# The second pair of output-projection tiles made of seven block products in place of eight

## The chip, the cores and the metric

The kernel runs on one core of one Trainium2 chip. The metric is the time of one execution on the device in microseconds (us), as the median of several runs. The engines are named as the profile names them: PE is TensorE (PEld its weight loads), DVE is VectorE, ACT is ScalarE, POOL is GpSimd and SP is SyncE, which only issues DMAs here.

## The reference

One decoder layer for 512 prompt tokens and 8 sample tokens (520 columns), in float32. What bears on this case is the end of the token mixer, where the merged branches go through the output projection onto the residual, and the norm behind it:

```python
x = x + (jax.nn.sigmoid(ga) * y_a + jax.nn.sigmoid(gb) * y_b) @ w_o
xn = rmsnorm(x, g2)
up = xn @ w_up
```

`w_o` is 1024 x 1024.

## The kernel before

**Tiles and slots.** Activations lie feature by feature: 8 blocks of 128 features (KT = 8) by 520 tokens (TOK), in two halves of 260 (HALF). A weight tile of 128 outputs by 1024 inputs is one slot; slots run in one fixed order and alternate between two buffers of everything (`raw`, `whi`, `wlo`, and the PSUM tiles `out_ps`, each with one bank for each half). Each float32 product is made of three fp32r products, high x high, high x low and low x high, so a slot takes 8 blocks x 3 x 2 halves = 48 matmuls of 128 x 128 by 260 columns. SP loads the raw weights of a slot; ACT's `split` rounds them to `whi`; DVE's `low` subtracts to get `wlo`; PE runs the slot (`tile`); DVE or ACT empties the PSUM tile (semaphores `evac`).

**The seven-product pairs.** Four tiles of the branch before (the gate slots of class `Pair`, two pairs) are already made this way: two output tiles, two halves of the inputs and two halves of the tokens make a 2 x 2 by 2 x 2 block product, which takes seven block products (`product`, 4 blocks x 3 = 12 matmuls each) in place of eight. For this DVE makes four sums of weight blocks (`weight_sums` into `wsum`), ACT and DVE split seven factors into high and low (`factor_hi`, `factor_low`, semaphores `factor_hi` and `factor_lo`), and x needs four combinations of its quarters (`tf`, split into `th` and `tl`). The products go to several PSUM places and DVE adds them up. The tile that follows a pair, `branch_tile`, takes its weights in two halves as places in `whi` and `wlo` come free.

**The output projection.** Its slots are S_WO to S_WO + 7, one for each output block j. Its input is `merged` (float32, 8 blocks), split block by block into `mh` and `ml`; the first tile waits for these block by block. For each j, DVE adds PSUM and residual (`xres`) into `x1`, which gives the semaphore s_x1; ACT multiplies by a gain into `x2h`, DVE makes the low part `x2l`. Between the two DVE makes the low weights of slot j + 2.

**POOL beside it.** POOL loads small constants for the next stage, stores `out_conv_old`, makes `sconv` of four operations, and then for each j squares `x1` (`sqa`) and adds it up (`acc`). After 6 of 8 blocks of the first tile of the next stage (S_UP), PE sums `acc` over the partitions (`norm_sums`) and so waits for all eight.

Order on each engine is the order of its program; there is no scheduler.

## Time and profile before

| | |
|---|---|
| median of 3 runs | 907.07 us (906.8 to 907.54) |
| the profiled execution, whole time | 906.57 us |
| its span, first to last instruction | 904.4 us |
| PE busy | 896.8 us, 99% |
| DVE busy | 548.9 us, 61% |
| ACT busy | 373.4 us, 41% |
| POOL busy | 136.2 us, 15% |

The span is what the trace covers; the profiled execution's own time is 2.17 us longer. Start times in rows count from the start of the span. Busy PE is not PE at its peak, since matmuls are pipelined; the distance from one matmul's start to the next tells the pace.

### The profile page before, as it was taken

How to read it: one execution, taken by the hardware profiler on the slowest of the kernel's cores; microseconds unless marked ns; L12 is line 12 of the kernel's file. 1: busy time of each engine (PE TensorE's matmuls, PEld its weight loads, DVE VectorE, ACT ScalarE, POOL GpSimd, SP SyncE). 2: the span in 40 equal slices, each digit the busy share in tenths (PEclk: the TensorE clock that was granted, in tenths of full speed). 3: DMA queues.
4: the chain of work that ended last, by engine and by line, in shares of the span. 5: the costliest groups of instructions: out<-in, count | busy, mean ns of one | idle time of the engine just before them, and what ended most of it. 6: DMA issues, size and time to landing. Idle time of an engine off the chain costs nothing.

```text
span 904.4 us, 19408 instructions
## 1 busy us (share of the span) xinstructions
PE 896.8 (99%) x7378; PEld 892.7 (99%) x7378; DVE 548.9 (61%) x863; ACT 373.4 (41%) x580; POOL 136.2 (15%) x182
## 2 busy tenths in 40 slices
PE   9999999999999999999999999999999999999997
PEld 9999999999999999999999999999999999999997
DVE  7895774442885444396755687777777777433234
ACT  7545434535863323243332344444444444322222
POOL 0682000011541111000006700000000000000001
PEclk9999999999999999999999999999999999999999
DMA  6332252234862222222254222222222222323322
GB/s 212 120 115 94 70 219 87 71 122 139 316 243 71 75 83 75 93 92 71 93 208 125 93 78 92 89 90 93 93 93 93 93 93 88 98 86 96 96 85 95
DMA packets 31489, 100.30 MB, mean 111 GB/s; under 512 B 4668, under 2 KB 7260, under 8 KB 31192
## 3 DMA queue, kind: packets, MB, share of 16 engines
q1 hardware_dynamic: 29256, 92.96, 30.7%
q0 software_dynamic: 1472, 5.72, 2.1%
q10 hardware_dynamic: 720, 1.04, 0.3%
q8 instruction: 29, 0.48, 0.2%
q14 instruction: 12, 0.10, 0.0%
HBM read 92.37 MB, written 7.35 MB: 110 GB/s over the span
## 4 chain that ended last, share of the span: by engine, by line
PE 91%; POOLq 3%; issue 3%; DMA 1%; POOL 1%; DVEq 0%; ACT 0%; DVE 0%; SPq 0%; ACTq 0%
PE out L1713 86%; PE trp L1713 2%; POOLq L1691 2%; PE aux L1713 1%; POOLq L1689 1%; PE trp L1745 1%; DMA cwb<-in_conv_wb 1%; DMA raw_pair<-in_w_slots 0%; PE aux L1902 0%; POOL y L1704 0%; POOL out_conv_old L1675 0%; POOL sct L1679 0%; DVEq L1530 0%; ACT whi L527 0%; POOLq L1682 0%
## 5 line engine op out<-in xcount | busy, mean ns | idle before, releaser
L971 DVE TENSOR_TENSOR wlo<-raw_pair,whi 128x1024 fp32r<-128x1024 f32 (+1 forms) x139 | 174.5, 1255 | 193.1 <-ACT whi L527 192.8
L527 ACT ACTIVATE whi<-raw_pair 128x1024 fp32r<-128x1024 f32 (+3 forms) x156 | 155.0, 997 | 251.8 <-PE out L1713 249.3
L1713 PE MATMUL out<-xh,whi 128*128 128x260 f32 x728 | 152.7, 288 | 0.0
L1713 PE MATMUL out<-xh,wlo 128*128 128x260 f32 x728 | 148.6, 283 | 0.0
L1713 PE MATMUL out<-xl,whi 128*128 128x260 f32 x728 | 148.5, 283 | 0.0
L1713 PE MATMUL out<-x2h,wlo 128*128 128x260 f32 x704 | 142.0, 283 | 0.0
L1713 PE MATMUL out<-x2h,whi 128*128 128x260 f32 x704 | 142.0, 283 | 0.0
L1713 PE MATMUL out<-x2l,whi 128*128 128x260 f32 x704 | 141.8, 283 | 0.0
L1713 PEld LDWEIGHTS out<-xh,whi 128*128 128x128 f32 x728 | 113.5, 189 | 0.5
L1713 PEld LDWEIGHTS out<-xh,wlo 128*128 128x128 f32 x728 | 113.1, 189 | 0.0
L1713 PEld LDWEIGHTS out<-xl,whi 128*128 128x128 f32 x728 | 113.0, 188 | 0.0
L1713 PEld LDWEIGHTS out<-x2h,whi 128*128 128x128 f32 x704 | 108.7, 189 | 0.1
L1713 PEld LDWEIGHTS out<-x2h,wlo 128*128 128x128 f32 x704 | 108.6, 189 | 0.0
L1713 PEld LDWEIGHTS out<-x2l,whi 128*128 128x128 f32 x704 | 108.3, 188 | 0.0
L1713 PE MATMUL out<-acth,whi 128*128 128x260 f32 (+2 forms) x338 | 70.7, 283 | 0.0
L1713 PE MATMUL out<-acth,wlo 128*128 128x260 f32 (+2 forms) x338 | 70.7, 283 | 0.0
L1713 PE MATMUL out<-actl,whi 128*128 128x260 f32 (+2 forms) x338 | 70.5, 283 | 0.0
L1489 DVE TENSOR_TENSOR up<-out,rbc 128x520 f32<-128x520 f32 x44 | 30.9, 702 | 42.1 <-PE out L1713 42.0
L1713 PEld LDWEIGHTS out<-acth,whi 128*128 128x128 f32 x338 | 53.1, 189 | 0.0
L1713 PEld LDWEIGHTS out<-acth,wlo 128*128 128x128 f32 x338 | 53.2, 189 | 0.0
L1713 PEld LDWEIGHTS out<-actl,whi 128*128 128x128 f32 x338 | 53.1, 188 | 0.0
L1697 POOL COPY nconv<-up 128x10 f32 x44 | 8.9, 203 | 242.9 <-DVEq L1490 242.9
(311 smaller groups left out, 1474.8 us busy)
## 6 DMA issues: line engine op xcount, KB each, us to landing
raw_pair<-in_w_slots SPq DMA_DIRECT2D x123, 512.0 KB, 3.3
raw_pair<-in_w_dn SPq DMA_DIRECT2D x16, 448.0 KB, 3.3
c_ring<-in_C_state SPq DMA_DIRECT2D x8, 512.0 KB, 4.9
row<-scratch SPq DMA_DIRECT2D x8, 512.0 KB, 5.9
out_C_sample<-c_ring SPq DMA_DIRECT2D x8, 512.0 KB, 4.2
raw_pair<-in_w_dn SPq DMA_DIRECT2D x8, 512.0 KB, 3.6
xres<-in_x_all POOLq DMA_DIRECT2D x1, 1560.0 KB, 6.9
x<-in_x_all SPq DMA_DIRECT2D x5, 260.0 KB, 6.5
```

The lines of the kernel that those rows point to most:

```text
L527: return act.activation(out, in_, func, **kw_)
L971: TT(wlo[p][:, 0:width], raw[p][:, 0:width], whi[p][:, 0:width].bitcast(F32), ALU.subtract)\
L1489: TT(both(up[t][:, 2:2 + TOK]), out2(n), both(rbc2[:, :]), ALU.mult).then_inc(evac[n.c % 2], 1)
L1689: pool.drain()
L1691: pool.drain()
L1697: pool.tensor_copy(nconv[:, i * 2 + t, :], up[t][:, SEQ:2 + TOK]).then_inc(s_nc, 1)
L1713: return pe.matmul(*a, **k)
L1745: m = pe.transpose(trp[b.c % 2][:, c, :], ftmp[b.c % 2][:, c * P:(c + 1) * P], ident[:, :])
```

## The change

Output tiles j = 2 and 3 (slots S_WO + 2 and + 3) become a pair of seven products (`OutPair`). Tiles 0, 1 and 4 to 7 stay as they were, tile 4 (slot S_WO + 4) with its weights in halves (`halves_tile`, which is `branch_tile` with its inputs as arguments). The input combinations are made anew, from the fp32 tiles of `merged`: four differences of 4 blocks x 260 columns on DVE (`merged_difference`), their high parts on ACT (`merged_combination_hi` into `mth`), their low parts on DVE (`merged_combination_low` into `tl`). The first difference and its high part lie inside the last gate pair, the three others behind it, ahead of the sum of tile 0. The loops of the projection are written out on PE, DVE and ACT. On SP, the loads of S_WO + 4 and + 5 wait for the factors made of the buffers that they overwrite. POOL's program stays the same.

```diff
+        class OutPair(Pair):
+            def __init__(self):
+                self.q = (KT - PLAIN) // 2
+                self.j = 2
+                self.n = [At(S_WO + 2 + t) for t in range(4)]
+                self.t0, self.t1 = self.n[0].c % 2, self.n[1].c % 2
+                self.p1, self.p6 = (trp[t][:, :, :].rearrange("p a b -> p (a b)")[:, 0:HALF] for t in range(2))
+                self.p5, self.p7 = (aux[:, t, 0:HALF] for t in range(2))
+                r0, r1 = raw[self.t0], raw[self.t1]
+                self.a11, self.a12, self.a21, self.a22 = r0[:, 0:HW], r0[:, HW:], r1[:, 0:HW], r1[:, HW:]
+                self.factor = (self.a11, self.a12, wsum[:, 3, :], wsum[:, 1, :], wsum[:, 0, :], wsum[:, 2, :], self.a22)
+
+        pair_o = OutPair()
...
-            load_slots(S_WO, S_DN)
+            load_slots(S_WO, S_WO + 4)
+            sp.wait_ge(s_sw, 4 * pair_o.q + 4)
+            sp.wait_ge(s_pl, 7 * pair_o.q + 2)
+            sp.dma_start(raw[pair_o.t0][:, :], wp[S_WO + 4]).then_inc(w_loaded[pair_o.t0], 16)
+            sp.wait_ge(s_pl, 7 * pair_o.q + 7)
+            sp.dma_start(raw[pair_o.t1][:, :], wp[S_WO + 5]).then_inc(w_loaded[pair_o.t1], 16)
+            load_slots(S_WO + 6, S_DN)
...
+            def merged_combination_hi(r, at):
+
+                act.wait_ge(s_bt, 4 + at)
+                A(mth[r][:, :, :], tf[:, r, :, :]).then_inc(s_th, 1)
...
                 if last:
                     split(At(S_WO + 1))
+                    merged_combination_hi(0, 1)
                 else:
                     next_factors_hi(pairs_w[q + 1])
                 merged_hi(pr.j + 1)
...
+            def out_pair(pr):
+                q, n = pr.q, pr.n
+                act.wait_ge(w_loaded[pr.t0], n[0].half(1) * 16)
+                act.wait_ge(done, n[0]())
+                factor_hi(pr, 0)
+                factor_hi(pr, 1)
+                second_hi(0)
+                act.wait_ge(s_sw, 4 * q + 4)
+                act.wait_ge(done, n[1]())
+                factor_hi(pr, 2)
+                factor_hi(pr, 3)
+                act.wait_ge(s_pd, 6 * q + 1)
+                factor_hi(pr, 4)
+                second_hi(1)
+                A(wtmp[1], pr.p1).then_inc(s_or, 1)
+                act.wait_ge(s_pd, 6 * q + 2)
+                factor_hi(pr, 5)
+                act.wait_ge(s_pd, 6 * q + 3)
+                act.wait_ge(w_loaded[pr.t1], n[1].half(1) * 16)
+                factor_hi(pr, 6)
+                act.wait_ge(w_loaded[pr.t0], n[2].half(1) * 16)
+                act.wait_ge(s_pd, 6 * q + 5)
+                A(whi[pr.t0][:, 0:HW], raw[pr.t0][:, 0:HW]).then_inc(s_nh, 1)
+                act.wait_ge(s_pd, 6 * q + 6)
+                A(whi[pr.t0][:, HW:], raw[pr.t0][:, HW:]).then_inc(w_hi, 3)
+                split(n[3])
+
+            merged_combination_hi(2, 2)
+            merged_combination_hi(1, 3)
+            merged_combination_hi(3, 4)
+            out_pair(pair_o)
+            second_hi(2)
+            second_hi(3)
...
+            def merged_quarter(k, h):
+
+                return merged[:, k * KT // 2:(k + 1) * KT // 2, h * HALF:(h + 1) * HALF]
+
+            def merged_difference(r, a, b):
+
+                TT(tf[:, r, :, :], a, b, ALU.subtract).then_inc(s_bt, 1)
+
+            def merged_combination_low(r, at):
+
+                dve.wait_ge(s_th, 4 + at)
+                TT(tl[:, r, :, :], tf[:, r, :, :], mth[r][:, :, :].bitcast(F32), ALU.subtract).then_inc(s_tl, 1)
+
...
                 if last:
                     low(At(S_WO))
+                    merged_difference(0, merged_quarter(0, 1), merged_quarter(0, 0))
                     merged_low(pr.j)
                 else:
...
+                dve.wait_ge(s_x2h, j + 1)
+                STT(x2l[:, j, :], x1[:, j, :], gains[:, 2, j:j + 1], x2h[:, j, :].bitcast(F32),
+                    ALU.mult, ALU.subtract).then_inc(s_x2, 1)
+
+            def first_sum(n, j):
+
+
+                return TT(both(x1[:, j, :]), out2(n), both(xres[:, j, :]), ALU.add).then_inc(evac[n.c % 2], 1)
+
+            def first_result():
+
+                dve.drain()
+                dve.nop().then_inc(s_x1, 1)
+
+            def out_pair(pr):
+                q, n, j = pr.q, pr.n, pr.j
+                part = lambda t, h: x1[:, j + t, h * HALF:(h + 1) * HALF]
+                rest = lambda h: xres[:, j + 1, h * HALF:(h + 1) * HALF]
+                ready(At(S_WO))
+                first_sum(At(S_WO), 0)
+                first_result()
+                merged_combination_low(0, 1)
+                merged_combination_low(2, 2)
+                factor_low(pr, 0)
+                factor_low(pr, 1)
+                weight_sums(pr)
+                ready(At(S_WO + 1))
+                first_sum(At(S_WO + 1), 1)
+                first_result()
+                factor_low(pr, 2)
+                second_low(0)
+                factor_low(pr, 3)
+                merged_combination_low(1, 3)
+                factor_low(pr, 4)
+                factor_low(pr, 5)
+                merged_combination_low(3, 4)
+                second_low(1)
+                dve.wait_ge(s_xrest, 16)
+                dve.wait_ge(s_pd, 6 * q + 3)
+                first_sum(n[0], j)
+                factor_low(pr, 6)
+                dve.wait_ge(s_or, 1)
+                dve.drain()
+                TT(part(0, 0), part(0, 0), wtmp[1], ALU.add)
+                dve.wait_ge(s_pd, 6 * q + 4)
+                TT(wtmp[0], wtmp[1], pr.p6, ALU.add)
+                dve.wait_ge(s_nh, q + 1)
+                TT(wlo[pr.t0][:, 0:HW], raw[pr.t0][:, 0:HW], whi[pr.t0][:, 0:HW].bitcast(F32), ALU.subtract).then_inc(s_nl, 1)
+                dve.wait_ge(s_pd, 6 * q + 5)
+                dve.drain()
+                TT(wtmp[1], wtmp[0], pr.p5, ALU.add)
+                dve.wait_ge(w_hi, n[2](1))
+                TT(wlo[pr.t0][:, HW:], raw[pr.t0][:, HW:], whi[pr.t0][:, HW:].bitcast(F32), ALU.subtract).then_inc(w_lo, 3)
+                dve.wait_ge(s_pd, 6 * q + 6)
+                dve.drain()
+                TT(wtmp[0], wtmp[0], pr.p7, ALU.add)
+                TT(part(0, 1), part(0, 1), wtmp[1], ALU.add)
+                first_result()
+                low(n[3])
+                ready(n[1])
+                TT(part(1, 0), rest(0), wtmp[0], ALU.add)
+                TT(part(1, 1), rest(1), wtmp[0], ALU.add)
+                dve.drain()
+                TT(part(1, 0), part(1, 0), out_ps[pr.t1][:, 0, 0:HALF], ALU.add).then_inc(evac[pr.t1], 1)
+                TT(part(1, 1), part(1, 1), pr.p5, ALU.add)
+                first_result()
+                second_low(2)
+                second_low(3)
+
+            dve.drain()
+            merged_difference(2, merged_quarter(1, 1), tf[:, 0, :, :])
+            merged_difference(1, merged_quarter(1, 1), merged_quarter(0, 1))
+            dve.drain()
+            merged_difference(3, merged_quarter(1, 0), tf[:, 2, :, :])
             dve.wait_ge(s_xres, 16)
-            wo_step(0)
-            dve.wait_ge(s_xrest, 16)
-            with dve.Fori(1, KT // 2) as i:
-                wo_step(i)
+            out_pair(pair_o)
+            for j in range(4, KT):
+                n = At(S_WO + j)
+                ready(n)
+                first_sum(n, j)
+                first_result()
+                low(n.plus(2))
+                second_low(j)
 
             def hidden_low(i):
 
@@ -1956,7 +2103,7 @@
                 pe.wait_ge(s_u2, q + 1)
...
             tile(At(S_WO + 1), mh, ml)
-            with pe.Fori(1, 4) as i:
-                for t in range(2):
-                    tile(At(S_WO + t, i, 2), mh, ml)
+
+            def merged_product_quarter(k, h):
+
+                part = (slice(None), slice(k * KT // 2, (k + 1) * KT // 2), slice(h * HALF, (h + 1) * HALF))
+                return mh[part], ml[part]
+
+            def merged_combination(r):
+
+                return mth[r][:, :, :], tl[:, r, :, :]
+
+            def out_pair(pr):
+                n = pr.n
+                product(pr, 0, pr.p1, *merged_product_quarter(0, 0)).then_inc(s_pd, 1)
+                pe.wait_ge(evac[pr.t0], n[0].half(1))
+                product(pr, 1, out_ps[pr.t0][:, 0, 0:HALF], *merged_product_quarter(1, 0)).then_inc(s_pd, 1)
+                product(pr, 2, out_ps[pr.t0][:, 1, 0:HALF], *merged_product_quarter(1, 1)).then_inc(s_pd, 1)
+                pe.wait_ge(s_tl, 4 + 2)
+                product(pr, 3, pr.p6, *merged_combination(2)).then_inc(s_pd, 1)
+                product(pr, 4, pr.p5, *merged_combination(0)).then_inc(s_pd, 1)
+                pe.wait_ge(s_tl, 4 + 3)
+                product(pr, 5, pr.p7, *merged_combination(1)).then_inc(s_pd, 1)
+                pe.wait_ge(s_tl, 4 + 4)
+                pe.wait_ge(evac[pr.t1], n[1].half(1))
+                product(pr, 6, out_ps[pr.t1][:, 0, 0:HALF], *merged_combination(3)).then_inc(done, 2)
+
+            out_pair(pair_o)
+            halves_tile(pair_o, mh, ml)
+            for j in range(5, KT):
+                tile(At(S_WO + j), mh, ml)
```

On DVE, this stood from the last operation of the branch to the low part of tile 1 of the projection (`x_94<-out,xres` is the sum of a tile, `wlo_119<-raw_pair,whi_117 128x1024` the low weights of a slot, `ml` the low part of a block of `merged`):

```order
L1339 TENSOR_TENSOR ml<-merged,mh 128x520 [waits merged_hi]
L1456 TENSOR_TENSOR x_94<-out,xres 128x520 [waits slots_done,residual_loaded]
L971 TENSOR_TENSOR wlo_119<-raw_pair,whi_117 128x1024 [waits w_hi]
L1461 SCALAR_TENSOR_TENSOR x2l<-x_94,gains,x2h 128x520 [waits x2_hi]
L1456 TENSOR_TENSOR x_94<-out,xres 128x520 [waits slots_done]
L971 TENSOR_TENSOR wlo_118<-raw_pair,whi_116 128x1024 [waits w_hi]
L1461 SCALAR_TENSOR_TENSOR x2l<-x_94,gains,x2h 128x520 [waits x2_hi]
```

And this stands there now, behind `ml<-merged,mh` and a first `tf<-merged,tf`, up to the factor that the third product takes (`tf` is a difference of `merged`, `tl<-tf,mth` its low part, `wlo ... 128x512` the low part of a factor, `wsum` the weight sums):

```order
L1430 TENSOR_TENSOR tf<-merged 128x1040
L1430 TENSOR_TENSOR tf<-merged,tf 128x1040
L1540 TENSOR_TENSOR x_94<-out,xres 128x520 [waits slots_done,residual_loaded]
L1435 TENSOR_TENSOR tl<-tf,mth_114 128x1040 [waits x_combinations_hi]
L1435 TENSOR_TENSOR tl<-tf,mth_116 128x1040 [waits x_combinations_hi]
L1411 TENSOR_TENSOR wlo_123<-raw_pair,whi_121 128x512 [waits factor_hi] x2
L1417 TENSOR_TENSOR wsum<-raw_pair 128x512 [waits w_loaded0,w_loaded1]
L1419 TENSOR_TENSOR wsum<-wsum,raw_pair 128x512
L1420 TENSOR_TENSOR wsum<-raw_pair 128x512
L1422 TENSOR_TENSOR wsum<-raw_pair,wsum 128x512
L1540 TENSOR_TENSOR x_94<-out,xres 128x520 [waits slots_done]
L1411 TENSOR_TENSOR wlo_122<-wsum,whi_120 128x512 [waits factor_hi]
```

Ahead of the sum of tile 0 stand three differences (two of them shown), and between the sums of tiles 0 and 1 two low parts of combinations, two factors and the four weight sums, where one `wlo` of a slot and one `x2l` stood.

Farther on DVE, from the factor of the fifth product to the two halves of the low weights of slot S_WO + 4 (`wlo ... [waits branch_half_hi]` and `[waits w_hi]`), all new:

```order
L1411 TENSOR_TENSOR wlo_123<-wsum,whi_121 128x512 [waits factor_hi] x2
L1435 TENSOR_TENSOR tl<-tf,mth_117 128x1040 [waits x_combinations_hi]
L1534 SCALAR_TENSOR_TENSOR x2l<-x_94,gains,x2h 128x520 [waits x2_hi]
L1540 TENSOR_TENSOR x_94<-out,xres 128x520 [waits products_done,residual_rest_loaded]
L1411 TENSOR_TENSOR wlo_122<-raw_pair,whi_120 128x512 [waits factor_hi]
L1576 TENSOR_TENSOR x_94<-x_94,ftmp_127 128x260 [waits out_product_copied]
L1578 TENSOR_TENSOR ftmp_127<-ftmp_127,trp 128x260 [waits products_done]
L1580 TENSOR_TENSOR wlo_123<-raw_pair,whi_121 128x512 [waits branch_half_hi]
L1583 TENSOR_TENSOR ftmp_127<-ftmp_127,aux 128x260 [waits products_done]
L1585 TENSOR_TENSOR wlo_123<-raw_pair,whi_121 128x512 [waits w_hi]
```

The factor of the seventh product (`wlo_122<-raw_pair,whi_120 128x512`) comes behind a low part, an `x2l` and a sum; the first half of the low weights of S_WO + 4 comes two more operations later.

On PE the tiles of the projection followed each other; this is the start of one in the loop (`out<-mh,whi`: high inputs, high weights):

```order
L1981 ISA
L1720 REGISTER_ALU [waits w_lo]
L1713 MATMUL out<-mh,whi_117 128x260 [waits bank_emptied1]
L1713 MATMUL out<-mh,whi_117 128x260
L1713 MATMUL out<-ml,whi_117 128x260 x2
L1713 MATMUL out<-mh,wlo_119 128x260 x2
```

Now the seventh product stands there, twelve matmuls on the last combination, of which the first three and the last are shown, and then tile 4:

```order
L1860 MATMUL out<-mth_117,whi_120 128x260 [waits factor_lo,bank_emptied0,x_combinations_lo]
L1860 MATMUL out<-tl,whi_120 128x260
L1860 MATMUL out<-mth_117,wlo_122 128x260
...
L1860 MATMUL out<-tl,whi_120 128x260
L1860 MATMUL out<-mth_117,wlo_122 128x260
L1860 MATMUL out<-mh,whi_121 128x260 [waits bank_emptied1,branch_half_lo]
```

A product of 12 matmuls now waits for a factor of its own, and the tile behind it for the first half of its low weights.

## Rows read from the trace of the kernel before

**Rows 1.** First part of the page: busy time of the engines.

```profile
PE 896.8 (99%) x7378; PEld 892.7 (99%) x7378; DVE 548.9 (61%) x863; ACT 373.4 (41%) x580; POOL 136.2 (15%) x182
```

**Rows 2.** Busy time over the projection's eight tiles (from:to length, engines' busy us, clock).

```profile
467.40:513.50 46.10, 46.10 (x386) 46.10 (x385) 27.30 (x25) 14.21 (x16) 29.77 (x23) 1.00 0.47 140
```

**Rows 3.** Timeline of PE: first matmuls of S_WO and of S_UP (start, length).

```profile
467.39 0.41 PE L1713 MATMUL out<-mh,whi 128*128 128x260 f32 x2
...
513.52 0.40 PE L1713 MATMUL out<-x2h,whi 128*128 128x260 f32 x2
```

**Rows 4.** Timeline of DVE: in the gate pairs, sums, factors, weight sums.

```profile
430.14 0.43 DVE L1408 TENSOR_TENSOR gtmp<-gtmp,out 128x260 f32<-128x260 f32 x1
...
441.69 1.29 DVE L1344 TENSOR_TENSOR wlo<-raw_pair,whi 128x512 fp32r<-128x512 f32 x2
442.89 0.69 DVE L1350 TENSOR_TENSOR wsum<-raw_pair 128x512 f32<-128x512 f32 x1
443.67 0.69 DVE L1352 TENSOR_TENSOR wsum<-wsum,raw_pair 128x512 f32<-128x512 f32 x1
...
445.06 0.69 DVE L1355 TENSOR_TENSOR wsum<-raw_pair,wsum 128x512 f32<-128x512 f32 x1
```

**Rows 5.** Combinations of x, high on ACT, low on DVE (ns min/median/max).

```profile
L527 ACT ACTIVATE th<-tf x4: 1053/1059/1062, 397.1 to 404.4; 128x1040 fp32r<-128x1040 f32 x4
L1327 DVE TENSOR_TENSOR tl<-tf,th x4: 1233/1234/1236, 404.5 to 410.5; 128x1040 fp32r<-128x1040 f32 x4
```

**Rows 6.** Timeline of DVE in the first two projection tiles (idle time before, and releaser).

```profile
473.42 0.70 DVE L1456 TENSOR_TENSOR x<-out,xres 128x520 f32<-128x520 f32 x1 [2.60 <-PE out L1713]
...
475.59 0.75 DVE L1461 SCALAR_TENSOR_TENSOR x2l<-x,gains,x2h 128x520 fp32r<-128x520 f32 x1
479.12 0.70 DVE L1456 TENSOR_TENSOR x<-out,xres 128x520 f32<-128x520 f32 x1 [2.77 <-PE out L1713]
480.21 1.25 DVE L971 TENSOR_TENSOR wlo<-raw_pair,whi 128x1024 fp32r<-128x1024 f32 x1 [0.39 <-ACT whi L527]
481.39 1.34 DVE L1461 SCALAR_TENSOR_TENSOR x2l<-x,gains,x2h 128x520 fp32r<-128x520 f32 x1
```

**Rows 7.** Timeline of POOL beside the projection.

```profile
477.42 2.07 POOL L1675 DMA_DIRECT2D out_conv_old<-cst  x1 [7.98 <-DMA cwb<-in_conv_wb]
479.43 0.95 POOL L1678 TENSOR_TENSOR sconv<-cst,cwb 128x352 f32<-128x352 f32 x1
480.25 1.92 POOL L1679 TENSOR_TENSOR sct<-cst,cwb 128x352 f32<-128x352 f32 x1
487.40 1.20 POOL L1681 TENSOR_TENSOR sconv<-sconv,cwb 128x352 f32<-128x352 f32 x1 [5.23 <-issue]
488.75 0.94 POOL L1683 TENSOR_TENSOR sconv<-sconv,sct 128x352 f32<-128x352 f32 x1
...
490.30 1.05 POOL L1688 TENSOR_TENSOR sqa<-x 128x520 f32<-128x520 f32 x1
491.50 1.31 POOL L1690 TENSOR_TENSOR acc<-acc,sqa 128x520 f32<-128x520 f32 x1
492.95 1.85 POOL L1688 TENSOR_TENSOR sqa<-x 128x520 f32<-128x520 f32 x1
...
514.66 1.05 POOL L1688 TENSOR_TENSOR sqa<-x 128x520 f32<-128x520 f32 x1 [1.71 <-DVEq L1457]
```

**Rows 8.** Timeline of DVE beside the rows of POOL from 490 us.

```profile
491.75 2.13 DVE L971 TENSOR_TENSOR wlo<-raw_pair,whi 128x1024 fp32r<-128x1024 f32 x1 [0.28 <-ACT whi L527]
493.81 1.55 DVE L1461 SCALAR_TENSOR_TENSOR x2l<-x,gains,x2h  x1
```

**Rows 9.** Sixth part of the page: the load of a slot (us to landing).

```profile
raw_pair<-in_w_slots SPq DMA_DIRECT2D x123, 512.0 KB, 3.3
```

**Rows 10.** Busy time at the span's end, PE idle (granted clock after the engines).

```profile
900.00:901.00 1.00, 0.00 (x0) 0.00 (x0) 0.95 (x4) 0.00 (x0) 1.00 (x2) 1.00 0.43 139
901.00:902.00 1.00, 0.00 (x0) 0.00 (x0) 0.00 (x0) 0.00 (x0) 0.21 (x1) 0.53 1.06 352
```

More of the change, by code:

```diff
@@ L60 @@
 PLAIN = 4
+OUT_PAIRS = 1
 HW = KT * P // 2
@@ L174, in hybrid_layer @@
         assert Q0 + 41152 + 16 * HW <= 165952
+        mth = [at("mth0", [P, KT // 2, HALF], Q0 + 2 * XB, F32R)]
+        mth += [at(f"mth{r}", [P, KT // 2, HALF], 4 * XB + XB // 4 * (r - 1), F32R) for r in range(1, 4)]
+        assert 4 * XB + 3 * XB // 4 <= F0
         acth = at("acth", [P, FT, TOK], Q0, F32R)
@@ L386, in hybrid_layer @@
         s_gs = sem("gate_sigmoids")
+        s_or = sem("out_product_copied")
         s_nh = sem("branch_half_hi")
@@ L860, in _, with second_hi @@
                 ay_pair(pr)
-            with act.Fori(0, KT // 2) as i:
-                for t in range(2):
-                    n = At(S_WO + t, i, 2)
-                    split(n.plus(2))
-                    apart()
-                    act.wait_ge(s_x1, i * 2 + (t + 1))
-                    A(x2h[:, i * 2 + t, :], x1[:, i * 2 + t, :], scale=gains[:, 2, bass.ds(i * 2 + t, 1)]).then_inc(s_x2h, 1)
+            def second_hi(j):
+                act.wait_ge(s_x1, j + 1)
+                A(x2h[:, j, :], x1[:, j, :], scale=gains[:, 2, j:j + 1]).then_inc(s_x2h, 1)
+            def out_pair(pr):
[31 more added lines that the diff above has]
+            for j in range(4, KT):
+                split(At(S_WO + j + 2))
+                second_hi(j)
             def up_step(i, first=False, last=False):
@@ L1448, in _ @@
                 ay_pair(pr)
-            def wo_step(i):
-                for t in range(2):
-                    n = At(S_WO + t, i, 2)
-                    j = i * 2 + t
-                    ready(n)
-                    TT(both(x1[:, j, :]), out2(n), both(xres[:, j, :]), ALU.add).then_inc(evac[n.c % 2], 1)
-                    dve.drain()
-                    dve.nop().then_inc(s_x1, 1)
-                    low(n.plus(2))
-                    dve.wait_ge(s_x2h, i * 2 + (t + 1))
-                    STT(x2l[:, j, :], x1[:, j, :], gains[:, 2, bass.ds(j, 1)], x2h[:, j, :].bitcast(F32),
-                        ALU.mult, ALU.subtract).then_inc(s_x2, 1)
@@ new lines, in _ @@
+            dve.drain()
[3 more added lines that the diff above has]
+            merged_difference(3, merged_quarter(1, 0), tf[:, 2, :, :])
+            dve.wait_ge(s_xres, 16)
+            out_pair(pair_o)
+            for j in range(4, KT):
+                n = At(S_WO + j)
[4 more added lines that the diff above has]
+                second_low(j)
@@ L1967, in branch_tile @@
                     w = slice(k * P, (k + 1) * P)
-                    for wt, x in ((whi[pr.t0], hah), (whi[pr.t0], hal), (wlo[pr.t0], hah)):
+                    for wt, x in ((whi[pr.t0], hi), (whi[pr.t0], lo), (wlo[pr.t0], hi)):
                         for a in range(2):
                             m = MM(out_ps[pr.t0][:, a, 0:HALF], wt[:, w], x[:, k, a * HALF:(a + 1) * HALF],
-                                   start=k == 0 and wt is whi[pr.t0] and x is hah, stop=k == KT - 1 and wt is wlo[pr.t0])
+                                   start=k == 0 and wt is whi[pr.t0] and x is hi, stop=k == KT - 1 and wt is wlo[pr.t0])
                 m.then_inc(done, 1)
@@ L1975, in _ @@
                 gate_pair(pr)
-                branch_tile(pr)
+                halves_tile(pr, hah, hal)
                 tile(pr.n[3], hah, hal)
@@ L1980, in _ @@
             tile(At(S_WO + 1), mh, ml)
-            with pe.Fori(1, 4) as i:
-                for t in range(2):
-                    tile(At(S_WO + t, i, 2), mh, ml)
+            def merged_product_quarter(k, h):
[21 more added lines that the diff above has]
+                tile(At(S_WO + j), mh, ml)
             def norm_sums(ready, count, signal):
```

4 lines of the change are left out of this document (3 added, 1 removed).

## The prediction

> **What bounds the kernel now.** I read the first part of the page first: PE is busy for 896.8 us of 904.4, and no other engine above 61% [rows 1]. So every matmul taken away shortens the kernel by its pace, and every time that PE has to wait lengthens it. Then I looked at the stretch of the change, the eight projection tiles: PE is busy in all of it at full clock, DVE for 27.3 of 46.1 us, ACT for 14.2, POOL for 29.8 [rows 2]. The tiles run from 467.39 to 513.52 us [rows 3], 46.13 us for 8 x 48 matmuls: 0.120 us each, 5.77 a tile, 1.44 for a product of 12. PE never waits there, because DVE's work lies in the shadow of a tile: it waits 2.6 to 2.8 us for PE before each sum shown [rows 6]. That slack is what the change spends, and it has to be added up in order of time, since DVE does its work in the order of its program.
>
> **What is taken away.** Two tiles are 96 matmuls, seven products 84. 12 x 0.120 = 1.44 us less on PE, 0.16% of the kernel. Everything else must be hidden.
>
> **Durations on DVE.** A factor or weight sum of 512 columns takes 0.69 us; two in a row take 1.29, so the next one starts 0.09 before the record of the one before ends; with a drain between, it starts 0.08 or 0.09 behind the end (442.89 + 0.69 against 443.67); the four weight sums take 2.86 from first start to last end [rows 4]. A piece of 1040 columns takes 1.23, so 1.15 in a row [rows 5]; nothing in the trace shows a difference of `merged`, but it is the same operation on as many columns as that low part, and I take the same. A sum of a tile takes 0.70, an `x2l` 0.75 [rows 6], a sum of 260 columns 0.43 [rows 4].
>
> **DVE and POOL get in each other's way.** This is the second thing to read. An `x2l` takes 0.75 us at 475.59, but 1.34 at 481.39, where POOL's `sct` runs until 482.17 [rows 6, 7]. From 490 us on each waits for the other: `acc` runs alone until 492.81 in 1.31 us; the low weights begun at 491.75 take 2.13 and end at 493.88, 1.07 behind it; `sqa` begun at 492.95 takes 1.85 in place of 1.05 and ends at 494.80, 0.92 behind that; the `x2l` then ends at 495.36 [rows 7, 8]. So one stands still until the other is through, then needs its own time less about 0.15. Sums that read PSUM go on beside POOL (0.70 at 479.12, with `sconv` from 479.43 in its usual 0.95) [rows 6, 7]. The Trainium skill ("SBUF — State Buffer", section "Who interferes with whom") has it as a rule: a VectorE instruction with two SBUF inputs contends with a GpSimd instruction that reads SBUF, and whoever is first holds the shared port for the whole instruction. By that rule, the trace agrees, nearly everything that this change adds to DVE can be stopped by POOL. Without the waiting the sum below would be +1.0 us, with it +7.0.
>
> **The sum, in order of time.**
> 1. Up to the end of the branch, one difference (1.15 on DVE, 1.06 on ACT [rows 5]) goes in ahead of the split of the last block of `merged`. That block's low part ends at about 470.9; PE wants it in its eighth step, 467.39 + 7 x 0.72 = 472.4. Hidden by 1.5 us; without that cover it would cost what is left of the 2.2.
> 2. Three differences (3.45 and two drains) keep DVE until 474.7. The sum of tile 0 follows to 475.3 (474.1 before) and gives the bank that product 2 of 7 needs from 480.4: hidden.
> 3. Two combination lows (2.3) and two factors (1.2) end at 479.0; the first factor is there at 478.4, and PE starts the pair at 467.39 + 2 x 5.77 = 478.92. Hidden by half a microsecond. ACT, with pieces of at most 1.06, stays ahead of DVE.
> 4. The four weight sums would take 478.9 to 481.8, but POOL's `sconv` and `sct` come at 479.4 [rows 7] and step in between: 483.0. The sum of tile 1 (to 483.7) and the factor follow, 484.5. PE has done two products by 478.92 + 2.88 = 481.8. **Wait of 2.7 us.** Third product at 484.5.
> 5. An `x2l`, a factor (485.7, in time for 486.0), a combination low (486.9), a factor (487.5; PE wants 487.4: **0.1 us**).
> 6. From 487.3 POOL is at work without a pause: the rest of `sconv`, then `sqa` and `acc` of tiles 0 and 1, each 0.9 to 1.3 us [rows 7]. DVE has a factor (488.8), a combination low (490.6), an `x2l` (492.1), the sum of tile 2 (492.7) and the last factor (493.8), every one but the sum behind one of POOL's. PE has ended product six at 490.4. **Wait of 3.5 us**; the seventh runs from 493.9 to 495.3.
> 7. Tile 4 needs the first half of its low weights, which stands behind a sum of two SBUF pieces (495.0, behind POOL) and one from PSUM (495.4), and itself behind POOL (496.7): **1.4 us**. Tile 4 starts at 496.75.
> 8. Its second half comes at 497.8, wanted at 499.6. Then DVE has two sums of 0.43, the low weights of tile 5 (1.22), two more sums with POOL's `sqa` and `acc` of tile 2 between, and at 503.1 the sum that gives back the bank that tile 5 needs; PE is free for it at 502.5: **0.7 us**.
>
> The waits are 2.7 + 0.1 + 3.5 + 1.4 + 0.7 = 8.4; less 1.44, **+7.0 us**. Behind tile 5 DVE catches up: the low weights of tile 6 come at 508.1, wanted at 508.9, and nothing later is short.
>
> **What costs nothing.** SP issues as many loads as before. That of tile 4 waits for the weight sums and goes at 483.1; at 3.3 to landing [rows 9] it is there at 486.4, and ACT takes it behind the fifth product, 489.2. That of tile 5 goes behind the last factor, 493.8, lands at 497.2 and is split at 498.3, just before DVE comes to it; the load of tile 6 is queued behind both and has ten microseconds. POOL's `sqa` and `acc` of tile 2 begin at 498.8 in place of 496.7, but POOL had 1.7 us to spare before its last block [rows 7] and less waits on it in the later tiles, so the wait for the norm's sum stays as it is.
>
> The profiled execution took 906.57 us: 913.5. The median of the runs is 0.50 above it: **914.0 us**.
>
> **The rivals.** What a measurement of this kernel can tell from no change is about 0.2%, 1.8 us.
> - **All is hidden** (3%, not slower). The third factor would have to be there at 481.8 and the seventh at 487.5, with no pause: 905.6 us, -0.16%, which is no difference. Against it: from 470.9 to the third factor DVE has 12.3 us of work of its own by the steps above (the weight sums at their 2.86) and 10.9 us of time. It decides for this rival if the five waits add up to less than 1.44 us; POOL's two operations in step 4 alone take most of that.
> - **DVE and POOL don't hold each other up** (6%). Then the waits are 1.5 (step 4), 0.1, and 0.8 (step 6), together 2.4: +1.0, 908.0 us, within the 0.2%. Rows 7 and 8 speak against it.
> - **POOL comes later** (18%). Between `sct` and the rest of `sconv` POOL stands for 5.2 us for a reason that the profile doesn't show [rows 7]; its `out_conv_old` was issued just before. If a busier DVE lengthens this by 1 to 3 us, POOL's work falls beside the seventh product's time and less before its factor: I get +5.9, +5.0 and +5.5 in place of +7.0 for 1, 2 and 3 us later, 3.0 for 8 us: 910 to 913 us.
> - **The clock falls** (15%). PE, busy 99% of the time before [rows 1], now stands for 2.7 and 3.5 us with some products between. At the end of the trace, where it has nothing left to do, the granted clock is still full (2.4 GHz) from 900 to 901 us and at 0.53 of full, that is at 1.2 GHz for most of it, in the next microsecond [rows 10]. At half the clock a matmul takes up to twice as long, so each microsecond of projection work done so costs up to another one, as far as PE and not DVE sets the pace: 2 to 3 us more for some 3 us of work, 916 to 917. The Trainium skill ("TensorE: Matmul & The Clock Gate", section "Why this matters for your kernels") says to avoid gaps of this kind between bursts, since one idle stretch brings the half clock back; no row here shows it at work in the middle of a kernel.
> - **As forecast** (58%), 911.5 to 915.5.
>
> **How the numbers follow.** Bounds of what no row shows: a difference between 0.69 (half the columns) and 1.34 (the slowest `x2l`) changes step 4 by at most 1.4 down and 0.3 up. The range reaches down into the third rival and up over the fourth: 910.0 to 917.5 leaves out the first two (9%), some 3% of the third and some 5% above. Slower by over 0.2%: 58 + 18 + 15 = 91%; within 0.2%: the first two, 8%; faster by more than 0.2%: 1%, since 1.44 us is less than 1.8 and nothing else is taken away.
>
> **What would show it.** In the profile after: PE with an idle time of some 2.7 us before its third product and 3.5 before its seventh, both released by `wlo` factors of DVE; another of 1.4 before tile 4; first matmul of S_UP near 520.5 in place of 513.5. Weight sums stretched by `sconv` and `sct`; POOL's operations from 487 us in turn with DVE's. Products at 0.120 us a matmul. The prediction is wrong if DVE's factors come earlier than this list, by POOL being elsewhere, or if a matmul behind a wait takes longer than 0.120.

## The result and the profile after

The changed kernel takes **916.84 us** (median of 6 runs, 915.94 to 919.63) against 906.84 us (6 runs, 906.64 to 907.54) for the kernel before: a ratio of 1.0115, 95% interval 1.0103 to 1.0126, or 10.0 us slower. The forecast was 914.0, +7.0. The profiled execution took 915.94 us; it is the fastest of the six.

The same views as before the change. First part of the page, with 12 matmuls fewer on PE and 28 us more busy time on DVE than in [rows 1], and the busy time over the projection, first matmul of S_WO to first matmul of S_UP, in answer to [rows 2]:

```profile
PE 898.1 (98%) x7366; PEld 892.3 (98%) x7366; DVE 577.0 (63%) x889; ACT 379.0 (41%) x591; POOL 135.6 (15%) x182
...
466.98:523.34 56.36, 48.33 (x375) 46.60 (x373) 52.78 (x50) 19.97 (x27) 30.65 (x23) 0.97 0.37 114
```

The projection grew from 46.13 us [rows 3] to 56.36, by 10.23; it also began 0.4 us sooner. DVE, which was busy 27.3 us of 46.1, is now busy 52.8 of 56.4, and each of the longer waits of PE ends with an operation of DVE. The timeline of PE, where it starts again after a wait (start, length, idle time before and its releaser), and from the view of waits over the same stretch the largest entry (us in total, times, longest):

```profile
485.23 0.39 PE L1860 MATMUL out<-mh,whi 128*128 128x260 f32 x1 [3.08 <-DVE wlo L1411]
490.46 0.40 PE L1860 MATMUL aux<-mth,whi 128*128 128x260 f32 x1 [0.41 <-DVE wlo L1411]
497.18 0.36 PE L1860 MATMUL out<-mth,whi 128*128 128x260 f32 x1 [3.24 <-DVE wlo L1411]
505.14 0.48 PE L1860 MATMUL out<-mh,whi 128*128 128x260 f32 x2 [0.54 <-DVE x L1596]
511.69 0.51 PE L1860 MATMUL out<-mh,whi 128*128 128x260 f32 x2 [0.55 <-DVE wlo L1038]
```

```profile
PE out L1860 <- DVE wlo L1411: 6.3, 2, 3.2
```

Line 1411 is `factor_low`: the two long waits are those before the third and the seventh product. Beside them, DVE and POOL, one timeline each (start, length):

```profile
477.40 2.92 DVE L1411 TENSOR_TENSOR wlo<-raw_pair,whi 128x512 fp32r<-128x512 f32 x2
480.25 1.33 DVE L1417 TENSOR_TENSOR wsum<-raw_pair 128x512 f32<-128x512 f32 x1
...
484.49 0.69 DVE L1411 TENSOR_TENSOR wlo<-wsum,whi 128x512 fp32r<-128x512 f32 x1
485.10 1.35 DVE L1534 SCALAR_TENSOR_TENSOR x2l<-x,gains,x2h 128x520 fp32r<-128x520 f32 x1
486.37 1.42 DVE L1411 TENSOR_TENSOR wlo<-wsum,whi 128x512 fp32r<-128x512 f32 x1
...
488.87 3.24 DVE L1411 TENSOR_TENSOR wlo<-wsum,whi 128x512 fp32r<-128x512 f32 x2
492.03 2.09 DVE L1435 TENSOR_TENSOR tl<-tf,mth 128x1040 fp32r<-128x1040 f32 x1
494.05 1.78 DVE L1534 SCALAR_TENSOR_TENSOR x2l<-x,gains,x2h 128x520 fp32r<-128x520 f32 x1
```

```profile
478.81 0.95 POOL L1825 TENSOR_TENSOR sconv<-cst,cwb 128x352 f32<-128x352 f32 x1
479.63 1.39 POOL L1826 TENSOR_TENSOR sct<-cst,cwb 128x352 f32<-128x352 f32 x1
484.97 0.92 POOL L1828 TENSOR_TENSOR sconv<-sconv,cwb 128x352 f32<-128x352 f32 x1 [3.95 <-issue]
486.04 1.21 POOL L1830 TENSOR_TENSOR sconv<-sconv,sct 128x352 f32<-128x352 f32 x1
...
490.00 1.56 POOL L1837 TENSOR_TENSOR acc<-acc,sqa 128x520 f32<-128x520 f32 x1
491.70 1.32 POOL L1835 TENSOR_TENSOR sqa<-x 128x520 f32<-128x520 f32 x1
493.17 2.10 POOL L1837 TENSOR_TENSOR acc<-acc,sqa 128x520 f32<-128x520 f32 x1
```

What to see: two factors take 2.92 in place of 1.29, two later ones 3.24; an `x2l` 1.35 and 1.78 in place of 0.75; and the ends interlock (POOL's `sqa` ends at 493.02, the combination low begun at 492.03 at 494.12, 1.10 behind it). The pause of POOL behind `sct` is 3.95 us long, where [rows 7] had 5.23, so POOL is back at 484.97. The windows behind the first long wait show the granted clock (the figure behind the five engines, ahead of the DMA share) fall to half, 1.2 GHz; matmuls then start 0.217 us apart in place of 0.120:

```profile
485.00:486.00 1.00, 0.77 (x4) 0.77 (x5) 1.00 (x2) 1.00 (x3) 0.89 (x1) 0.74 0.83 279
486.00:487.00 1.00, 1.00 (x7) 1.00 (x6) 1.00 (x2) 0.86 (x3) 0.96 (x1) 0.50 0.44 176
487.00:488.00 1.00, 1.00 (x6) 0.80 (x5) 1.00 (x2) 0.00 (x0) 0.86 (x3) 0.50 0.00 0
488.00:489.00 1.00, 1.00 (x6) 1.00 (x6) 1.00 (x2) 0.63 (x1) 1.00 (x1) 0.55 0.00 0
489.00:490.00 1.00, 1.00 (x9) 0.83 (x8) 1.00 (x1) 0.00 (x0) 0.86 (x1) 1.00 0.06 16
```

The whole account, from the starts of the products and tiles on PE, each start less the one before and less its own time at full clock (1.44 us a product, 5.77 a tile):

| product or tile | start | us lost before it | forecast |
|---|---|---|---|
| 1st, 2nd product | 478.81, 480.47 | 0.3 + 0.2 | 0 |
| 3rd product | 485.23 | 3.3 | 2.7 |
| 4th (3rd at half clock) | 487.94 | 1.3 | 0 |
| 5th (4th at half clock until 489, then a wait) | 490.46 | 1.1 | 0.1 |
| 6th | 492.26 | 0.4 | 0 |
| 7th | 497.18 | 3.5 | 3.5 |
| tile 4 | 498.67 | 0.05 | 1.4 |
| tile 5 | 505.14 | 0.7 | 0.7 |
| tile 6 | 511.69 | 0.8 | 0 |
| S_UP | 523.34 | 0.1 | 0 |

Together 11.7 us; less the 1.44 of the twelve matmuls, 10.2. This is the account of the fastest execution; what the slower ones lose beyond it no trace shows.

### The profile page after: what moved, and what is told of

Its sections match the earlier page's. It is cut to its first block, busy times and chain, and to the rows that moved or that the text cites. A ratio compares the mean times of both kernels' runs of the same rounds, so it can differ in the third digit from the quotient of the medians.

```text
span 914.1 us, 19343 instructions
## 1 busy us (share of the span) xinstructions
PE 898.1 (98%) x7366; PEld 892.3 (98%) x7366; DVE 577.0 (63%) x889; ACT 379.0 (41%) x591; POOL 135.6 (15%) x182
## 4 chain that ended last, share of the span: by engine, by line
PE 92%; DVE 3%; issue 2%; DVEq 1%; DMA 1%; ACT 0%; POOL 0%; POOLq 0%; SPq 0%; ACTq 0%
PE out L1860 87%; PE trp L1860 2%; PE aux L1860 1%; PE trp L1892 1%; DMA raw_pair<-in_w_slots 1%; DVE wlo L1411 1%; DVE wlo L1038 1%; DVE x2l L1534 1%; DVE tl L1435 0%; DVEq L1544 0%; PE aux L2049 0%; ACT whi L554 0%; POOL y L1851 0%; DVEq L1418 0%; DVEq L1575 0%
## 5 line engine op out<-in xcount | busy, mean ns | idle before, releaser
L554 ACT ACTIVATE whi<-raw_pair 128x1024 fp32r<-128x1024 f32 (+2 forms) x158 | 154.9, 984 | 240.1 <-PE out L1860 227.6
```

The costliest lines, as they stand in the source:

```text
L554: return act.activation(out, in_, func, **kw_)
```

## The experiments

Two theories stood at the start. **A**: DVE is stopped by POOL, operation by operation, and this is nearly all of the cost. **B**: DVE simply has too much work ahead of the products, and POOL is a small part. A third, **C**, gives a share to PE's clock. The kernel before ran beside each group, with medians of 906.51, 906.46 and 906.63 us.

### POOL without its arithmetic

```diff
-  pool.tensor_tensor(sconv...), (sct...), sconv + wb(3), sconv + sct
-  8 x (pool.tensor_tensor(sqa, x1, x1), pool.tensor_tensor(acc, acc, sqa))
+  pool.memset(sconv[:, :, :], 0.5); pool.memset(acc[:, :], 8.0)
```

Made of the changed kernel (e1) and of the kernel before (e2), so that `conv_new` and the sum of the norm are constants in both; e3 is e1 with the store of the old convolution states issued behind the norm.

> The changed kernel without POOL's 20 operations beside the projection (sconv's four, the squares and sums of x1; memsets stand in their place, so the second norm and the sample tokens' convolution are left out). POOL's store of conv_old stays. Port theory (DVE operations with two SBUF inputs stand still while POOL works, and this is most of the loss): the waits shrink to 1.5 before the third product, 0.1, and 0.8 before the seventh, perhaps 0.7 more for what the store holds up; +1.0 to +1.7 us against the kernel before, near 908. Work theory (DVE has simply too much to do, POOL or not): +6 us or more, 913 and up.

> Control: the kernel before with the same 20 operations of POOL left out. PE never waits for DVE in its projection, so both theories expect no more than the end of the wait for the norm's sum: -0.2 to -0.5 us.

> As e1, with the store of conv_old issued behind the projection as well. If this DMA holds DVE's first factor (1.35 us in place of 0.69 in the profile after), that factor takes 0.69 here and 1.3 to 1.4 in e1, and this kernel is 0.5 to 0.7 us faster than e1. If it was anything else, the factor stays at 1.35 and the times agree.

Measured: e1 907.11 us, ratio 1.0004 (0.9995 to 1.0013); e2 905.98, 0.9990 (0.9981 to 0.9999); e3 907.17, 1.0005 (0.9996 to 1.0014). The change costs 10.0 us with POOL's 20 operations and 1.1 us without: A holds for 8.9 of the 10 us, and B for what is left, waits of 2.0 us less the 1.44. Waits of e1 over the projection, and its DVE at the places where the changed kernel's was stretched:

```profile
PE out L1850 <- DVE wlo L1411: 2.0, 2, 1.4
```

```profile
478.07 1.28 DVE L1411 TENSOR_TENSOR wlo<-raw_pair,whi 128x512 fp32r<-128x512 f32 x2
479.28 0.68 DVE L1417 TENSOR_TENSOR wsum<-raw_pair 128x512 f32<-128x512 f32 x1
...
485.91 1.28 DVE L1411 TENSOR_TENSOR wlo<-wsum,whi 128x512 fp32r<-128x512 f32 x2
```

Every operation shown has its length from [rows 4]. The busy time of DVE over the projection divides the same way. In e1, then in e2:

```profile
467.64:514.96 47.32, 45.34 (x375) 44.84 (x374) 36.62 (x50) 19.88 (x27) 4.55 (x6) 1.00 0.44 137
```

```profile
467.84:513.98 46.14, 46.14 (x387) 46.14 (x386) 21.33 (x25) 14.21 (x16) 4.55 (x6) 1.00 0.46 141
```

The change gives DVE 36.6 - 21.3 = 15.3 us of work of its own. The rest of its busy time is standing still for POOL: 27.3 - 21.3 = 6.0 us before, all of it in the slack, and 52.8 - 36.6 = 16.2 us after. I had thought that the store of the old states, which POOL issues at 476.81, is what stretches the two factors from 477.40; in e1 it is issued at the same place beside them and they take 1.28, and e3, where it comes behind the norm, has the same time as e1. That idea fell.

### PE kept busy while it waits

```diff
+  filler(24, pr.p7)                          # ahead of the third product
+  filler(24, out_ps[pr.t1][:, 0, 0:HALF])    # ahead of the seventh
```

The changed kernel with 48 matmuls whose results nobody reads, in the two long waits.

> The changed kernel with 24 matmuls without use (2.9 us) before the third product and 24 before the seventh, where PE waits 3.2 us each time; they go to PSUM places that the next product starts anew. Clock theory (the clock at half behind the first wait costs 2 us or more of the 10): the granted clock stays full and the time falls to 913 to 914.5 and varies less. Port theory: the factors of DVE set the pace behind the wait, so the fastest runs stay within 0.5 us of 916; only the slower runs (918 to 919.6) go.

Measured: 915.78 us (915.75 to 917.03, 4 runs), ratio 1.0097 (1.0082 to 1.0113). The clock stays at full, as the windows of e4 show against the same ones above:

```profile
486.00:487.00 1.00, 1.00 (x11) 1.00 (x10) 1.00 (x2) 1.00 (x3) 0.97 (x1) 1.00 0.84 246
487.00:488.00 1.00, 1.00 (x10) 0.95 (x8) 1.00 (x2) 0.94 (x3) 0.88 (x1) 1.00 0.56 225
```

but PE then waits 0.87 us for its factor at the fourth product, where it waited for none, and 0.83 in place of 0.41 at the fifth. From the third product's start to the fifth's e4 loses 2.1 us at full clock, the changed kernel 2.4 with half of it at the lower one. So in this kernel C is true of the records and worth little in time: DVE would not have let PE go on sooner. By the times alone the share stays open: the medians differ by 1.1 us, the two intervals overlap, and the runs of 918 us and more, which the changed kernel had, are missing among four. Nor is the trace of e4 the plain counterpart of the one above. It is of the slowest of its four runs (917.03), in which the first two factors took 4.05 us and the second product waited 1.09 for one of them, and the matmuls put in held the third product for 0.3 us (its factor was there at 486.25, it started at 486.56).

### Another order on DVE

```diff
 first_sum(At(S_WO), 0)
-merged_combination_low(0, 1); merged_combination_low(2, 2)
-factor_low 0, 1; weight_sums
+weight_sums; factor_low 0, 1
+merged_difference(3); merged_combination_low(2, 2)
 ...
-second_low(0), second_low(1) between the factors
+second_low(0), second_low(1) behind tile 2
```

Weight sums first, the last difference behind the first two factors, each combination low just ahead of its product, the two `x2l` out of the pair: e5 with POOL as it is, e6 with POOL quiet as in e1 (so conv_new and the norm's sum are constants there too).

> The changed kernel with DVE's work in another order, POOL as it is: weight sums and factors first, a combination's difference and low part just before its product, both x2l of tiles 0 and 1 behind the seventh factor, the first half of the low weights of tile 4 ahead of the sums. Port theory: 1.4 us of x2l and what POOL stops them for leave the way to the seventh product, but the rest still waits for POOL: +5 to +8 us against the kernel before, 911.5 to 914.5. Order theory (the loss is that the operations stand in an unlucky order, not that POOL stops them): +0 to +2 us.

> e5 without POOL's 20 operations (the second norm and the sample tokens' convolution left out). Port theory and the count of matmuls: with neither POOL nor an unneeded operation on the way, PE waits at most 0.3 us: 1.1 to 1.4 us faster than the control e2, near 904.8. If PE still waits for 1 us or more, something else than DVE and POOL holds it (ACT's highs, loads).

Measured: e5 920.06 us, ratio 1.0153 (1.0139 to 1.0167), e6 908.89, 1.0029 (1.0018 to 1.0040): both worse than the order they replaced. My expectation was wrong at a place that I had not looked at. Timeline of DVE in e5, and the DMA issues from 468 to 480 us (KB each, us to landing):

```profile
477.62 1.38 DVE L1417 TENSOR_TENSOR wsum<-raw_pair 128x512 f32<-128x512 f32 x1 [3.25 <-DMA raw_pair<-in_w_slots]
```

```profile
xres<-in_x_all POOLq DMA_DIRECT2D x1, 1560.0 KB, 6.8
raw_pair<-in_w_slots SPq DMA_DIRECT2D x1, 512.0 KB, 7.1
```

The weight sums need the second raw block of the pair, and its load takes 7.1 us here, where the median is 3.3 [rows 9]. It is in flight together with `xres` (1560 KB), and the DMA engines are busy for 95 to 100% of 472 to 476 us, so they probably share them; the load of the same place takes 6.6 us in the kernel before and 6.9 in the changed one. DVE stands for 3.25 us, and the first factor, now behind the weight sums, is 4.5 us late for PE, in e6 2.4. The order of the change had the combination lows in just that time.

In e6 this is PE's only wait, and 2.4 less 1.44 is 1.0, where e6 lies 2.9 above e2. The rest is the clock. It fell to half behind the wait, and the first two products took 1.6 us more than their own time with nothing to wait for. The window of e6:

```profile
482.00:484.00 2.00, 2.00 (x12) 2.00 (x11) 2.00 (x2) 0.03 (x1) 0.00 (x0) 0.50 0.95 71
```

So C, small in the changed kernel, is more than half of the loss in e6, where no factor of DVE was late behind the wait.

### Squares on ACT

```diff
+  act: A(sq2[j % 2], x1[:, j, :], ACT.Square)         # in two buffers
-  pool: sqa = x1 * x1; acc = acc + sqa
+  pool: acc = acc + sq2[j % 2]
+  pool.wait_ge(s_pl, 7 * pair_o.q + 7)                # ahead of sconv
```

e7 adds this to e5, and the store last; e8 is the kernel before with ACT's squares and the store last.

> e5 with all of the kernel's work: the squares of x1 move from POOL to ACT (two buffers, POOL only adds them up), POOL's four operations on sconv wait until the seventh factor is made, and the store of conv_old goes behind the projection. Port theory: nothing of POOL stands beside the pair, so this comes near e6 with the wait for the norm's sum: -0.5 to -1.3 us against the kernel before. If POOL, started at 488 us, does not get through its eight sums by 513, PE waits for the norm: +1 to +4 us.

> Control of e7: the kernel before with the squares on ACT and the store of conv_old behind the projection, DVE's order and the eight plain tiles as they are. PE has no wait there but 0.2 us at the norm's sum: -0.4 to 0 us. A gain of e7 over this one is what the seven products bring.

Measured: e7 913.24 us, ratio 1.0074 (1.0060 to 1.0088), 6.8 us above the kernel before where I had expected a gain; e8 906.40, 1.0002 (0.9993 to 1.0011), so that the edit by itself costs nothing. The waits within the pair are gone but for the 1.9 us ahead of the first product; a new one stands behind it. Timeline of PE and of DVE in e7:

```profile
501.79 0.47 PE L1865 MATMUL out<-mh,whi 128*128 128x260 f32 x2 [2.75 <-DVE x L1601]
```

```profile
498.19 1.52 DVE L1598 TENSOR_TENSOR x<-xres,ftmp 128x260 f32<-128x260 f32 x1
499.63 1.51 DVE L1599 TENSOR_TENSOR x<-xres,ftmp 128x260 f32<-128x260 f32 x1
```

Two sums of 0.42 us take 1.5 each: POOL's work, put off until the seventh factor, now meets the pair's last sums, and with them the bank of tile 5. The two waits, 4.7 us, less 1.44 make 3.2 of the 6.8. Most of the rest is again the clock, at half behind each of them: 1.6 us more in the first two products and 1.6 in tile 5. A window of e7 behind the second:

```profile
502.00:504.00 2.00, 2.00 (x12) 2.00 (x12) 1.90 (x3) 1.96 (x3) 0.94 (x2) 0.55 0.00 0
```

### The store late, POOL otherwise as it is

```diff
-  pool.dma_start(outs["conv_old"], cst[:, :, 1, :])   # ahead of sconv
   pool.nop().then_inc(s_acc, 1)
+  pool.dma_start(outs["conv_old"], cst[:, :, 1, :])
```

> The changed kernel whole, but POOL issues the store of the old convolution states at the very end of its work, behind the norm's squares. Theory A (this store, issued just before sconv and sct, is what makes POOL stand for 3.95 us between sct and the rest of sconv in the changed kernel, and 5.2 before): the gap falls to about 1.3 us, POOL begins its second sconv near 482.5 in place of 484.97 and does its squares in 484 to 492; DVE is then stopped more before the third product (wait 4 to 6 us) and less before the seventh (1 to 2.5), and the sum stays within 2 us of the change as it was: 914 to 918 us. Theory B (the gap is only DVE holding the memory): the gap stays above 3 us and the time at 916 to 917.

Measured: 914.67 us (914.48 to 915.81, 4 runs), ratio 1.0091 (1.0076 to 1.0106). Timeline of POOL, then the longer waits of PE:

```profile
481.02 1.34 POOL L1827 TENSOR_TENSOR sconv<-sconv,cwb 128x352 f32<-128x352 f32 x1 [1.31 <-issue]
```

```profile
PE out L1860 <- DVE wlo L1411: 4.3, 2, 3.7
PE aux L1860 <- DVE wlo L1411: 1.1, 1, 1.1
```

The pause falls to 1.31 us (and is 1.31 in e7, e8, e11 and e12, which have the store last too): the store makes what is beyond that. POOL's work then comes four microseconds sooner, hits the stretch before the third product harder (3.7, just under the 4 to 6 that I expected) and leaves the seventh nearly free (0.6; I had said 1 to 2.5). The time falls by 2.2 of the 10 us: where in the pair POOL's work lies matters less than that it lies there.

### POOL held back, and the sums behind the last factor

```diff
+  pool.wait_ge(s_x1, 4)                     # ahead of sconv; squares on ACT, store last
```

```diff
-  second_low(0), second_low(1), first_sum(n[0], j) ahead of factor_low(pr, 6)
+  factor_low(pr, 6); first_sum(n[0], j); low weights of tile 4; sums; second_low(0..3) behind tile 2
```

e11 has the first edit, e10 the second with POOL quiet, e12 both. The start of DVE's order stays as in the change.

> The changed kernel without POOL's 20 arithmetic operations in the projection (conv_new and the norm's sum are constants), and on DVE the two x2l and the sum of tile 2 stand behind the seventh factor, the two sums with product one and six behind the first half of tile 4's low weights; the order up to the weight sums stays as in the change. To be held against 907.11 (the same without POOL, order of the change) and 905.98 (kernel before without POOL). Theory: what is left of the cost with POOL quiet is DVE's order, two waits of 2.0 us together, of which two x2l and one sum at 0.65 each are the larger part: 905.0 to 906.0 us, PE's waits for factors in the stretch together under 1.0 us, at last a small gain by the 1.44 us of matmuls. Rival: the waits come from the chain weights -> ACT -> DVE and not from what stands between: 906.8 to 907.4.

> The changed kernel with its DVE order, whole output. POOL holds all its arithmetic back until the sum of tile 3 (the pair is through), ACT makes the squares of the norm in two buffers so that POOL has only the eight additions left, and the store of the old states goes last. The kernel before with ACT's squares and the late store took 906.40. Theory (DVE stopped by POOL inside the pair is 9 of the 10 us): PE's waits before the third and seventh product fall to the values with POOL quiet (2.0 us together), and the time to 907.0 to 909.0 us. Rival (the work of POOL only moves, and stops DVE before tiles 5 to 7 instead): waits of 3 us and more behind the pair, 910 to 913.

> Both edits: POOL held back until the sum of tile 3 with ACT's squares and the late store, and DVE's x2l and sum behind the seventh factor. Whole output. Theory: 905.5 to 907.5 us, within 0.2% of the kernel before on either side, so that the change's 1.44 us are won at best and mostly eaten by what POOL does behind the pair. Rival as for the run before: 909 to 912.

Measured: e10 906.17 us, ratio 0.9995 (0.9986 to 1.0004); e11 911.07, 1.0040 (1.0027 to 1.0054); e12 909.11, 1.0029 (1.0016 to 1.0041). Waits of PE in e10, in e11 and in e12:

```profile
PE out L1850 <- DVE wlo L1411: 1.4, 1, 1.4
```

```profile
PE out L1874 <- DVE wlo L1426: 2.0, 2, 1.4
PE out L1874 <- DVE wlo L1053: 1.9, 1, 1.9
```

```profile
PE out L1874 <- DVE wlo L1053: 1.9, 1, 1.9
PE out L1874 <- DVE wlo L1426: 1.4, 1, 1.4
```

In e11 the waits in the pair are those of e1, 2.0 us, with the whole output made (the squares on ACT, POOL's other twelve operations behind the pair): moving POOL's work out does for the pair what leaving it out does. In e12 and e10 only the 1.4 before the third product is left. Both e11 and e12 lie above what I expected, by 2.1 and 1.6 us, and inside the range of the rival, through a wait of 1.9 at line 1053, the low weights of tile 7. The rival is right in that POOL's work moves and costs something behind the pair, but not in how: DVE isn't stopped by POOL there (these low weights take 1.23 us). ACT's squares of tiles 2 and 3 stand ahead of `x2h` of tile 4 and wait for a free buffer, until POOL, started late, has added the first two (5.3 us in e11's waits, ACT for POOL `acc`), and DVE's `x2l`, which stands 6.7 us for that `x2h`, and the low weights of tile 7 are queued behind. In e11 the clock takes another 1.5 (see the last section). 909.11 less this wait is 907.2, which would be 0.1% above the kernel before; no run shows it.

e10 is the best of the orders tried: 906.17 against 905.98 for the kernel before with the same work left out (e2). With no stop by POOL and no avoidable operation ahead of the last factor, the 1.44 us of matmuls are eaten by the 1.40 us before the third product.

## Why the prediction came out as it did

The sign, the engine, the two large waits and their cause were right; the size was short: 10.0 us against 7.0. The measured 916.84 lies above the 911.5 to 915.5 of "as forecast" and in the 916 to 917 of the rival "the clock falls". That the number fits that rival is largely chance: the rival gave the clock 2 to 3 us, e4 gives it about 1. Of the signs named, the waits before the third product (3.08) and the seventh (3.24) came, that before tile 4 did not, S_UP began at 523.34 in place of 520.5, and one of the signs of being wrong came too: matmuls 0.217 us apart behind a wait. By the account of starts above, the terms that were too small make up 4.6 us (0.5 in step 3, 0.6 in step 4, 2.3 in step 5, 0.4 and 0.8 behind steps 5 and 8), the one too large 1.4 (step 7).

- **Steps 1 and 2** (hidden): right; nothing waits before the pair, and with POOL quiet nothing does either.
- **Step 3** (factors in time by half a microsecond): off by 0.5 (0.3 and 0.2 us late). The term left out is POOL's share on the two factors, 2.92 us for 1.29; it had been counted on the weight sums alone.
- **Step 4** (wait of 2.7): 3.3, the mechanism as described, but `sconv` and `sct` stopped the second factor and the first weight sum, and not the middle of the sums. Its part without POOL was given as 1.5; e11, e12 and e10 show 1.40.
- **Steps 5 and 6**: the 3.5 before the seventh product came out as 3.5, partly by luck. The input that failed is "from 487.3 POOL is at work": POOL was back at 484.97, since `sct` ended 1.2 us sooner (481.02 for 482.17) and the pause behind it was 3.95 us and not the 5.2 that I carried over. The `x2l` and the factor of step 5 (0.75 and 0.69) took 1.35 and 1.42, the next two factors 3.24. So the 0.1 us of step 5 is the term that was mis-sized: with the half-clock stretch before it, 2.4 us were lost between the third and the fifth product, and 0.4 before the sixth.
- **Step 7** (1.4): 0.05. It was too large: the seventh product ran while DVE, with POOL now done (no operation after 495.27), made the sum and the low weights at their own pace.
- **Step 8** (0.7): 0.7. Then the low weights of tile 6, which I had in time by 0.8, took 2.12 beside POOL and came 0.8 us late.

**The rivals.** "DVE and POOL don't hold each other" was the sum for e1, +1.0 against +1.1 measured, waits 1.5 and 0.8 against 1.4 and 0.6: the working without POOL was right to a tenth or two. It fell as a forecast because they do hold each other. The Trainium skill has this as its rule ("SBUF — State Buffer", section "Who interferes with whom"). The runs agree, and the 8.9 us between the two differences (changed less before, e1 less e2) are its price here, with what the clock does behind the waits in it. "POOL comes later" went the other way: POOL came 2.3 us sooner. "The clock falls" happened, from about 485.5 to 488.9, but e4 shows no more than about 1 us for it in the medians, since the factors were not there much earlier. Behind the second long wait the clock stayed at full (1.00 from 497 to 500 us). The Trainium skill ("TensorE: Matmul & The Clock Gate", section "Why this matters for your kernels") warns of gaps between bursts of matmuls. The runs agree in part: the fall came behind one of the two long waits of the changed kernel and not behind the other, and it cost little there, because PE was not the engine that set the pace; in e6, e7 and e11, where it was, 1.5 to 3.2 us.

## What to carry to other kernels

Work that trades matmuls for operations of two SBUF inputs on DVE must be priced with POOL's program beside it: count the operations of POOL in the stretch, add their time to DVE's, and compare that sum with what PE leaves. Here DVE's own 36.6 us left PE waiting for 2.0 us; beside POOL they became 52.8, and PE's waits 7.8. A trade of 1.44 us on PE needs the whole chain, weight sums included, ahead of the first product that uses it; the 1.40 us before one factor ate it. Where nothing else is late behind a wait of PE, add what the clock may cost to the wait itself. Before an operation is moved earlier, look up when its load lands there, and don't carry a pause that no row explains over to a new schedule.

## What was not expected

- **POOL's pause behind its own DMA.** Between `sct` and the next operation POOL stands 5.23 us before, 3.95 after (3.94 in e5, 4.36 in e4), and 1.31 with the store of the old states at the end (e7, e8, e9, e11, e12). The store is thus the cause; why its length differs between the two kernels no run shows.
- **Two factors stretched ahead of `sconv`.** They take 2.92 us in the changed kernel, though the record of `sconv` begins only at 478.81, when both could have been through; with the same store and memsets behind it (e1) they take 1.28. In e4 and e5 too an operation of DVE that was over before the record of `sconv` began was stretched, the first factor to 1.35 us and the first weight sum to 1.38. Something of `sconv` seems to hold the memory before its record starts; that is a guess, no run takes it apart.
- **A load beside POOL's loads takes 7.1 us** in place of 3.3 (e5), and 6.6 already in the kernel before.
- **The clock after like waits.** Behind the wait of 1.9 us ahead of tile 7, e11 and e12 differ. The windows of e11, then of e12:

```profile
510.00:512.00 2.00, 0.83 (x6) 0.83 (x7) 2.00 (x2) 1.95 (x3) 1.84 (x2) 0.97 0.00 0
512.00:514.00 2.00, 2.00 (x11) 2.00 (x10) 1.86 (x3) 0.48 (x1) 1.84 (x2) 0.50 0.74 262
514.00:516.00 2.00, 2.00 (x13) 2.00 (x13) 2.00 (x2) 0.78 (x2) 1.14 (x1) 0.68 0.00 0
```

```profile
510.00:512.00 2.00, 1.82 (x15) 1.82 (x16) 2.00 (x3) 0.96 (x2) 1.84 (x2) 1.00 0.36 117
512.00:514.00 2.00, 2.00 (x19) 2.00 (x18) 1.86 (x2) 1.26 (x2) 1.14 (x2) 1.00 0.39 145
```

e11 runs at half clock for some 3 us, e12 not at all, and the projection takes 51.0 us in the one and 48.5 in the other, of which e11's second wait in the pair is 0.6 and tile 7 1.5 (7.4 us against 5.9). Why one wait was followed by the lower clock and the other not, no run here shows.
